# Hybrid encoder step on one core: expert rows added to the tokens on chip, instead of written to DRAM and gathered

## The chip, the core and the metric

The kernel runs on one core of a Trainium2 chip. The metric is the device time of one execution in microseconds (us). Beside it stands the span of a profiled execution, from its first to its last instruction. Engines: PE (TensorE), DVE (VectorE), ACT (ScalarE), POOL (GpSimd), SP (SyncE, which here only starts DMAs).

## What is computed

One layer for 256 prompt tokens, 64 sample tokens and 16 meta tokens of width 1024, all float32: a projection, attention and a recurrent branch, a merge, a layer norm, and then a mixture of 16 experts of which each of the 320 tokens uses two. The change lies in the experts:

```python
combine = jnp.sum(jax.nn.one_hot(e_idx, N_EXPERTS, dtype=jnp.float32) * top_w[..., None], axis=1)
y = jnp.zeros((n, D_MODEL), jnp.float32)
for e in range(N_EXPERTS):
    h = jax.nn.silu(xt @ w_gate[e]) * (xt @ w_up[e])
    y = y + combine[:, e:e + 1] * (h @ w_down[e]).astype(jnp.float32)
...
z_p = layer_norm(ALPHA * z_p + hier_moe(z_p, ...), ln2_g[l], ln2_b[l])
```

The kernel computes each expert only for the tokens that chose it: `FIRST` = 64 rows, and `REST` = 32 more where an expert has more than 64 tokens (in this input two experts do, the ones numbered 1 and 10). Overflow beyond 96 rows has code of its own that this input doesn't enter.

## The kernel before

The program is written engine by engine, with semaphores; no scheduler orders it. Up to about 333 us it computes the projections, attention, the recurrence, the first layer norm (written to `z1_dram`) and the routing: for each expert a list of token numbers, `index_i`, and for each token the two places (`place`, `slot_i`) where its expert rows will stand.

Then come 15 rounds of a pipeline, one per expert, and a last one for expert 15 (`LAST`). `SP` streams each expert's three weight matrices of 2 MB (`w_gate`, `w_up`, `w_down`) into one of three slots: the loads of gate and up of expert i wait until PE has turned the hidden rows of expert i-3, the load of down until the down products of i-3 are done. `POOL` gathers 96 token rows per expert from DRAM (`gather`), three experts ahead.

In round i PE runs, in this order (`round_of` of the tensor block): `hidden(i)` (16 gate and 16 up products, float32, 64 rows each, two at a time on two column halves of the array), `down(i-1)` (8 products 512 wide), `turn(i+1)` (8 transposes of the next expert's token rows into banks 0 and 1), `rest(i)` if the expert has more than 64 tokens, and `turn_hidden(i)`. The hidden products use three banks in turn (`HB`). ACT does the tanh of the gate and, in `rows_out`, copies the down products out of PSUM and writes them to `y_dram` ("expert_rows") with two DMAs. DVE finishes the silu, copies the transposed rows (`columns`) and the transposed hidden rows (`hidden_columns`).

`y_dram` has 96 rows per item. Rows that no token writes must be zero or at least finite, so POOL zeroes them early, at about 71 to 82 us, with 22 DMAs (lines 731 to 735), and ACT zeroes expert 15's.

At the end POOL waits until all rows are written (lines 772 to 778) and gathers, for each of three token tiles, the two expert rows of each token (line 782); DVE adds them with their weights (line 1861). Expert 15 already takes another way: DVE builds a 128x384 matrix of weights that says which row belongs to which token (line 1852), PE turns it (`turn_own`) and multiplies it with expert 15's rows (`add_last`, line 1097, float32), and DVE adds the result (line 1878). Then comes the second layer norm, whose scale and shift rows (`ln2_g`, `ln2_b`, broadcast to 128 partitions) were loaded at about 313 us.

Of the kernel before, what the change touches and what calls it, by code (L numbers as in the profile page):

```python
# [7 lines left out]
F32 = mybir.dt.float32  # L8
F32R = mybir.dt.float32r
# [6 lines left out]
P = 128  # L16
# [59 lines left out]
def const_layout():  # L76

    cols, at = {}, 0
    for name, n in (("ident", P), ("ones", P), ("eps", 1), ("before", P), ("cos", 3 * HALF), ("sin", 3 * HALF),
                    ("iota_cap", CAP), ("iota_item", NITEM), ("iota_ov", NOV), ("expert", NE),  # L80
                    ("tie", 4), ("token", 3), ("valid", 3)):
# [8 lines left out]
def constants():  # L90
# [26 lines left out]
    put("eps", EPS)  # L117
    return c
# [131 lines left out]
def build(nc, t, outs):  # L250
    (y_prompt, y_sample, meta_k, meta_v, win_k, win_v, conv_p, h_p, new_k, new_v, conv_s, h_s) = outs
    with ExitStack() as ctx:
# [11 lines left out]
        with ExitStack() as under:  # L264
# [13 lines left out]
            attn_high = lower("attn_high", 4 * NTOK)  # L278
        slots = sb("expert_slots", [P, 3 * EXP])
# [6 lines left out]
        slot_i = sb("slot_i", [P, 2, 3], I32)  # L286
# [77 lines left out]
        xg = [ea.take(D) for _ in range(3)]  # L364
        xT = [ea.take(KD, CAP) for _ in range(3)]
        yo = [ea.take(512) for _ in range(3)]
        th_a, hid_a, hT_a = ea.take(256), ea.take(256), ea.take(256)
        th_b, hid_b, hT_b, yo_b = ea.take(P), ea.take(P), ea.take(P), ea.take(256)

        own_rows = [xg[2][:, 384 * k:384 * k + 384].rearrange("p (j h c) -> p j h c", h=2, c=FIRST) for k in range(2)]
        own_T = xT[2].rearrange("p k c -> p (k c)")[:, 0:NTOK]
        own_y = yo[2]
# [6 lines left out]

        fin = Area(slots, 2 * EXP, 3 * EXP)
        yg = [[fin.take(D) for _ in range(2)] for _ in range(3)]
# [24 lines left out]
        place = sm.take(12)  # L407
        own = sm.take(2, 3)
        idle = sm.take(1)
        exi, exo = rt.take(15), rt.take(15)  # L410
        g_top, tie_top, slot_f = rt.take(3), rt.take(3), rt.take(6)
# [21 lines left out]
        TB, HB, TH, YB, BB = banks[0:2], banks[2:5], banks[5], banks[6], banks[7]  # L433

        SUM = [[banks[0], banks[1]], [banks[3], banks[4]], [banks[5], banks[7]]]

        z1_dram = nc.dram_tensor("z1_rows", [NTOK, D], F32, kind="Internal")
        y_dram = nc.dram_tensor("expert_rows", [NITEM * CAP, D], F32, kind="Internal")
# [41 lines left out]
        zeroed, zero_out = sem("zeroed"), sem("zero_out")  # L480
# [10 lines left out]
        ya_full, ya_made = sem("ya_full"), sem("ya_made")  # L491
        y_out = [sem(f"y_out{i}") for i in range(3)]
# [3 lines left out]
        yb_full, yb_made, yb_out = sem("yb_full"), sem("yb_made"), sem("yb_out")  # L496
        y_written = sem("y_written")
        la_full, la_tanh, la_half, la_made = [sem(f"last_hidden_{n}") for n in ("full", "tanh", "half", "made")]
        lt_full, lt_made, ly_full, ly_made = [sem(f"last_{n}") for n in ("turned", "turned_made", "down", "down_made")]
# [184 lines left out]
        def _(pool):  # L684
# [46 lines left out]
            for i in range(NE):  # L731
                pool.dma_start(y_dram[CAP * i + FIRST:CAP * (i + 1), :], zeros).then_inc(zero_out, 16)
# [1176 lines left out]
```

## Time and profile before

| | us |
|---|---|
| median of 3 runs | 624.0 (620.52 to 624.64) |
| profiled execution, its own time | 623.38 |
| its span | 620.3 |
| PE busy / DVE / ACT / POOL | 513.8 / 250.8 / 149.7 / 66.9 |
| mean granted TensorE clock | 0.927 |

The profiled execution has 3.1 us outside its span. Busy shares are averages over very different stages: the expert rounds run from 340 to 597 us, and the last 20 us belong to DVE.

### The profile page before, as it was taken

What the parts mean: (1) busy time and instruction counts of PE and PEld (TensorE: products, weight loads), DVE (VectorE), ACT (ScalarE), POOL (GpSimd) and SP (SyncE); (2) the same over time, 40 slices, a digit from 0 to 9 for tenths busy, and PEclk for the clock granted to TensorE, in tenths of its full rate; (3) what the DMA queues carried; (4) which work ended last, traced back from release to release, by engine and by line L of the source; (5) the groups of instructions that cost most, each with busy time, mean ns of one, the idle gap of its engine ahead of it and who ended that gap; (6) DMA issues with size and microseconds to landing.
All of it is one profiled execution on the core that took longest, in us unless ns stands there. A gap on an engine that the chain in (4) does not pass through costs nothing.

```text
span 620.3 us, 9275 instructions
## 1 busy us (share of the span) xinstructions
PE 513.8 (83%) x3600; PEld 394.0 (64%) x3601; DVE 250.8 (40%) x526; ACT 149.7 (24%) x283; POOL 66.9 (11%) x87
## 2 busy tenths in 40 slices
PE   4789978999989897999952999889997799787740
PEld 1789965988989897988652555546554455354410
DVE  2936956789464444414334111111120121111187
ACT  3435349775534422001010010000000010000010
POOL 4151730000000000000004300000000000000210
PEclk9999979999999997999955899999998899999795
DMA  8227891424257645495293299999999999999642
GB/s 227 98 73 216 230 309 42 136 70 137 69 166 279 234 166 173 155 402 215 92 412 109 96 392 365 396 408 406 393 386 403 399 403 422 409 424 423 230 106 85
DMA packets 55212, 157.47 MB, mean 254 GB/s; under 512 B 3558, under 2 KB 36034, under 8 KB 51076
## 3 DMA queue, kind: packets, MB, share of 16 engines
q1 hardware_dynamic: 46464, 135.11, 58.0%
q0 software_dynamic: 4896, 13.92, 7.7%
q10 hardware_dynamic: 3812, 7.88, 3.4%
q8 instruction: 29, 0.48, 0.3%
q14 instruction: 11, 0.09, 0.0%
HBM read 145.10 MB, written 11.78 MB: 253 GB/s over the span
## 4 chain that ended last, share of the span: by engine, by line
PE 60%; DMA 21%; DVE 7%; issue 4%; ACT 4%; SPq 2%; DVEq 1%; POOL 0%; POOLq 0%; ACTq 0%
PE bank L1043 21%; DMA expert_slots<-in_w_up 11%; PE bank L850 7%; PE bank L851 7%; PE bank L852 7%; PE bank L1004 7%; DMA expert_slots<-in_w_branch_rnn 3%; PE bank L1036 2%; SPq L606 2%; DMA expert_slots<-in_w_in 2%; DMA z_rows<-work 2%; PE bank L831 2%; PE bank L832 1%; PE bank L833 1%; DVE work L1445 1%
## 5 line engine op out<-in xcount | busy, mean ns | idle before, releaser
L1043 PE MATMUL bank<-expert_slots,work 128*64 128x256 f32 (+3 forms) x1584 | 191.9, 415 | 30.8 <-DMA expert_slots<-in_w_gate 9.4
L1043 PEld LDWEIGHTS bank<-expert_slots,work 128*64 128x64 f32 (+1 forms) x1584 | 110.8, 139 | 100.7 <-issue 46.3
L850 PE MATMUL bank<-z_high,weights_high 128*128 128x320 f32 (+1 forms) x320 | 101.6, 317 | 7.6 <-DVE weights_low L555 5.2
L852 PE MATMUL bank<-z_high,weights_low 128*128 128x320 f32 (+1 forms) x320 | 100.9, 315 | 0.0
L851 PE MATMUL bank<-z_low,weights_high 128*128 128x320 f32 (+1 forms) x256 | 79.5, 310 | 0.0
L555 DVE TENSOR_TENSOR weights_low<-expert_slots,weights_high 128x1024 fp32r<-128x1024 f32 (+1 forms) x54 | 61.1, 1157 | 38.1 <-ACT weights_high L549 37.9
L850 PEld LDWEIGHTS bank<-z_high,weights_high 128*128 128x128 f32 x320 | 61.8, 193 | 9.1 <-DVE weights_low L555 5.9
L1802 DVE SCALAR_TENSOR_TENSOR work<-work,bank 128x256 f32<-128x256 f32 (+1 forms) x18 | 7.3, 407 | 147.3 <-ACT work L1350 141.5
L549 ACT CAST weights_high<-expert_slots 128x1024 fp32r<-128x1024 f32 (+1 forms) x54 | 52.2, 987 | 48.2 <-PE bank L852 15.9
L852 PEld LDWEIGHTS bank<-z_high,weights_low 128*128 128x128 f32 x320 | 61.7, 193 | 0.0
L851 PEld LDWEIGHTS bank<-z_low,weights_high 128*128 128x128 f32 x256 | 48.0, 188 | 0.0
L1350 ACT ACTIVATE work<-bank 128x256 f32<-128x256 f32 x16 | 6.2, 384 | 170.4 <-PE bank L1043 170.4
L1004 PE MATMUL bank<-expert_slots,work 128*128 128x256 f32 (+1 forms) x192 | 41.9, 380 | 1.1 <-DVE work L1669 1.1
L752 POOL DMA_INDIRECT work<-z_rows,index_i x16 | 14.8, 923 | 235.1 <-PE bank L1036 166.4
L1004 PEld LDWEIGHTS bank<-expert_slots,work 128*128 128x128 f32 (+1 forms) x192 | 32.9, 172 | 9.8 <-DVE work L1669 1.4
L1796 DVE COPY work<-bank 128x384 f32<-128x384 f32 x32 | 16.4, 553 | 51.0 <-PE bank L1036 51.0
L1036 PEld LDWEIGHTS bank<-const,work 96*128 96x128 f32 x128 | 15.8, 207 | 16.8 <-issue 16.8
L831 PE MATMUL bank<-weights_high,z_high 128*128 128x256 f32 (+1 forms) x72 | 21.2, 295 | 3.1 <-DVE z_low L1457 1.6
L1036 PE MATMUL bank<-const,work 96*128 96x96 f32 x128 | 18.5, 290 | 5.0 <-DMA work<-z_rows,index_i 5.0
L851 PE MATMUL bank<-rnn_low,weights_high 128*128 128x320 f32 x64 | 21.6, 337 | 0.0
L832 PE MATMUL bank<-weights_low,z_high 128*128 128x256 f32 (+1 forms) x72 | 21.0, 292 | 0.0
L833 PE MATMUL bank<-weights_high,z_low 128*128 128x256 f32 (+1 forms) x72 | 20.9, 290 | 0.0
(264 smaller groups left out, 567.5 us busy)
## 6 DMA issues: line engine op xcount, KB each, us to landing
expert_slots<-in_w_gate SPq DMA_DIRECT2D x16, 2048.0 KB, 22.4
expert_slots<-in_w_up SPq DMA_DIRECT2D x16, 2048.0 KB, 28.1
expert_slots<-in_w_down SPq DMA_DIRECT2D x15, 2048.0 KB, 24.0
expert_slots<-in_w_in SPq DMA_DIRECT2D x19, 1024.0 KB, 5.3
expert_slots<-in_w_branch_rnn SPq DMA_DIRECT2D x4, 1024.0 KB, 6.4
expert_slots<-in_w_out SPq DMA_DIRECT2D x4, 1024.0 KB, 5.1
expert_rows<-work ACTq DMA_DIRECT2D x30, 128.0 KB, 8.4
expert_rows<-work POOLq DMA_DIRECT2D x6, 384.0 KB, 9.6
```

Source lines behind the costliest of these rows:

```text
L549: nc.scalar.copy(high[n % AHEAD][:, ks, :], raw[u % RING][:, ks, cols]).then_inc(high_made, 1)
L555: nc.vector.tensor_tensor(low[u % RING][:, ks, cols], raw[u % RING][:, ks, cols], high[n % AHEAD][:, ks, :], ALU.subtract)\
L831: nc.tensor.matmul(b[0:n, 0:256], zh[:, k, z], wh[:, k, :], start=(k == 0), stop=False)
L832: nc.tensor.matmul(b[0:n, 0:256], zh[:, k, z], wl[:, k, :], start=False, stop=False)
L833: mm = nc.tensor.matmul(b[0:n, 0:256], zl[k // 4][:, k % 4, z], wh[:, k, :], start=False, stop=(k == KD - 1))
L850: nc.tensor.matmul(o, wh[:, k, :], xh, start=(k == 0), stop=False)
L851: nc.tensor.matmul(o, wh[:, k, :], xl, start=False, stop=False)
L852: mm = nc.tensor.matmul(o, wl[:, k, :], xh, start=False, stop=(k == kk - 1))
L1004: mm = nc.tensor.matmul(b[0:n, 256 * q:256 * q + 256], merged[:, k, P * j:P * j + n], w[:, k, :], start=(k == 0), stop=(k == KD - 1))
L1036: mm = nc.tensor.transpose(TB[h][:, k * CAP:k * CAP + CAP], cols[:, 4 * h + k, :], ident[0:CAP, 0:CAP])
L1043: mm = nc.tensor.matmul(bank[m * j:m * j + m, cols], lhsT(k), rhs(k, j), start=(k == 0), stop=(k == kk - 1))
L1796: cp = V.tensor_copy(xT[s][:, 4 * h:4 * h + 4, :], TB[h][:, 0:4 * CAP].rearrange("p (k c) -> p k c", c=CAP))
```

## The change

Nothing of the experts' output goes to DRAM any more. After the down product of an expert (two halves of 64 rows, one for each half of the 1024 columns, in one bank), ACT rounds the bank to float32r (`y_high`) and DVE makes the rounded difference (`low_part`), so that the sum of the two parts is nearly the float32 value. For each expert POOL makes a 0/1 matrix (`own_of`) that says which of its rows belongs to which token, from two rows per token (`slot_rows`) that PE and ACT spread over the partitions once. PE multiplies the 0/1 matrix with both parts (`add_tile`: for each of three token tiles 4 float32r products 512 wide on 64 partitions, the two row halves of the array alternating), into the two banks `SUM` for all tiles. DVE multiplies by the token's weight for this expert and adds to the residual rows (`add_sum`, two instructions per tile). The sums of expert i are made in round i+2.

To free banks, the hidden products now use one bank. To free memory, two of the three buffers of gathered token rows lie where the norm rows were, so the norm rows are fetched only after expert 14, as one row each, and spread by four PE products with one partition, before `hidden(LAST)`. In a round `turn(i+1)` now stands ahead of `down(i-1)`. In `rest` the down product takes 64-row tiles 512 wide (half of its rows are zeros) and its sums are made at once, PE waiting for DVE to the end.

```diff
-            for i in range(NE):
-                pool.dma_start(y_dram[CAP * i + FIRST:CAP * (i + 1), :], zeros).then_inc(zero_out, 16)
...
+            def own_of(i, s):
+                code = cst("lane")
+                for h in range(2):
+                    nc.gpsimd.tensor_scalar(same, slot_rows[:, 0, :], -float(CAP * i), code[:, h:h + 1], ALU.add, ALU.is_equal)\
+                        .then_inc(same_made, 1)
+                    nc.gpsimd.tensor_scalar(own[s][:, h, :], slot_rows[:, 1, :], -float(CAP * i), code[:, h:h + 1], ALU.add, ALU.is_equal)\
+                        .then_inc(same_made, 1)
+                    pool.wait_ge(same_made, 4 * own_of.n + 2 * h + 2)
+                    nc.gpsimd.tensor_tensor(own[s][:, h, :], own[s][:, h, :], same, ALU.add).then_inc(own_half, 1)
+                    pool.wait_ge(own_half, 2 * own_of.n + h + 1)
+                nc.gpsimd.tensor_copy(w_own[s], w_table[:, :, i]).then_inc(own_made, 1)
...
+            for i in range(1, NE):
+                if i + 2 < NE:
+                    pool.wait_ge(xt_full, i)
+                    gather(i + 2, (i + 2) % 3)
+                if i >= 3:
+                    pool.wait_ge(sum_free, 3 * (i - 2))
+                own_of(i, i % 3)
...
+            def add_tile(into, own_s, parts, j):
+                n = min(P, own_s.shape[-1] - P * j)
+                for w in range(2):
+                    for h in range(2):
+                        half = slice(FIRST * h, FIRST * h + FIRST)
+                        mm = nc.tensor.matmul(into[h][0:n, :], own_s[half, P * j:P * j + n], parts[half, w, :], start=(w == 0), stop=(w == 1))
+            def add(i, s, j):
+                if j == 0:
+                    pe.wait_ge(low_y, i + 1)
+                    pe.wait_ge(own_made, i + 1)
+                wait_past(pe, sum_free, 3 * i + j)
+                add_tile(SUM, own_first(s), y_parts, j).then_inc(sum_full, 1)
...
-                tiles(BB, slice(0, 256), lambda k: hT_b[:, REST * k:REST * k + REST],
-                      lambda k, j: w_down[s][:, k, 256 * j:256 * j + 256], KF, REST).then_inc(yb_full, 1)
+                tiles(BB, slice(0, 512), lambda k: hT_b[:, k, :],
+                      lambda k, j: w_down[s][:, k, 512 * j:512 * j + 512], KF, FIRST).then_inc(yb_full, 1)
+                pe.wait_ge(low_yb, b + 1)
+                pe.wait_ge(own_made, i + 1)
+                wait_past(pe, sum_free, summed)
+                for j in range(3):
+                    if j == 1:
+                        pe.wait_ge(rest_sum_free, 3 * b + 1)
+                    add_tile(REST_SUM[j], own[s][:, 1, :], yr_parts, j).then_inc(rest_sum_full, 1)
+                pe.wait_ge(rest_sum_free, 3 * b + 3)
...
+            for j in range(3):
+                add(LAST - 2, (LAST - 2) % 3, j)
             down(LAST - 1, 2, NE // 3 - 1)
+            for j in range(3):
+                add(LAST - 1, (LAST - 1) % 3, j)
...
+            pe.wait_ge(norm2_in, 32)
+            for i in range(2):
+                if i:
+                    pe.wait_ge(norm2_made, 2)
+                for h in range(2):
+                    nc.tensor.matmul(TB[h][:, :], ones[0:1, :], gb[0:1, i, 512 * h:512 * h + 512], start=True, stop=True)\
+                        .then_inc(norm2_full, 1)
             hidden(LAST, 0, NE // 3, la_full)
...
-                for h in range(2):
-                    act.dma_start(dst, yo[s][FIRST * h:FIRST * h + FIRST, :]).then_inc(y_out[s], 16)
+                nc.scalar.copy(y_parts[:, 0, :], YB[:, :]).then_inc(high_y, 1)
...
+            def low_part(parts, bank, high, n, made):
+                dve.wait_ge(high, n)
+                stt(parts[:, 1, :], bank[:, :], 1.0, parts[:, 0, :], ALU.mult, ALU.subtract).then_inc(made, 1)
+            def add_sum(into, full, count, s, j, done=None):
+                n = OUT_ROWS[j]
+                dve.wait_ge(full, count)
+                for h in range(2):
+                    half = rows[0:n, j, 512 * h:512 * h + 512]
+                    inst = stt(half, into[h][0:n, :], w_own[s][0:n, j:j + 1], half, ALU.mult, ALU.add)
...
-                alone(stt(rows[0:n, j, :], yg[j][k][0:n, :], weight[k][0:n, j:j + 1], rows[0:n, j, :], ALU.mult, ALU.add))
```

PE, one round of the loop over experts (the second of its three copies). Before: hidden, down, turn, and the load of the word that says whether the expert has a rest (`rest` and turn_hidden follow).

```order
L1043 MATMUL bank<-expert_slots,work 64x256 x32
L1043 MATMUL bank<-expert_slots,work 64x512 x8
L1036 MATMUL bank<-const,work 128x96 x8
L507 ISA
L507 TENSOR_LOAD ctrl_i
```

In the changed kernel (its line 1060 is `add_tile`, 1051 `tiles`, 1044 `turn`, 1099 `turn_hidden`):

```order
L1051 MATMUL bank<-expert_slots,work 64x256 x16
L191 REGISTER_ALU
L1060 MATMUL bank<-y_parts,own_tokens 128x512 x4
L1051 MATMUL bank<-expert_slots,work 64x256 x16
L191 REGISTER_ALU
L1060 MATMUL bank<-y_parts,own_tokens 128x512 x4
L1044 MATMUL bank<-const,norm_rows 128x96 x8
L1051 MATMUL bank<-expert_slots,work 64x512 x8
L191 REGISTER_ALU
L1060 MATMUL bank<-y_parts,own_tokens 128x512 x4
```

Three groups of 4 products are new, and the 8 transposes moved ahead of the down product.

PE, the body of `rest` in the same round, before:

```order
L1043 MATMUL bank<-expert_slots,work 32x128 x64
L1107 MATMUL bank<-const,work 128x128
L1043 MATMUL bank<-expert_slots,work 32x256 x16
L1116 UNCONDITIONAL_BRANCH
L1066 MATMUL bank<-const,work 128x128 x2
```

And in the changed kernel (line 1120 is the transpose, 1131 and 1133 are waits for DVE):

```order
L1051 MATMUL bank<-expert_slots,work 32x128 x64
L1119 REGISTER_ALU
L1120 MATMUL bank<-const,work 128x128
L1051 MATMUL bank<-expert_slots,work 64x512 x8
L191 REGISTER_ALU
L1060 MATMUL bank<-y_rest_parts,own_tokens 128x512 x4
L1131 ISA
L1060 MATMUL bank<-y_rest_parts,own_tokens 128x512 x4
L1060 MATMUL bank<-y_rest_parts,own_tokens 64x512 x4
L1133 REGISTER_ALU
L1137 UNCONDITIONAL_BRANCH
L1099 MATMUL bank<-const,work 128x128 x2
```

The 16 products 256 wide became 8 of 512, and three groups of sums with waits between and behind them stand ahead of the hidden transposes.

## Rows read from the trace of the kernel before

**Rows 1.** Page, the chain that ended last, by engine.
```profile
PE 60%; DMA 21%; DVE 7%; issue 4%; ACT 4%; SPq 2%; DVEq 1%; POOL 0%; POOLq 0%; ACTq 0%
```
**Rows 2.** Stretches: busy us per engine, PEclk, DMA share, GB/s.
```profile
440.00:455.00 15.00, 14.11 (x105) 7.83 (x101) 2.29 (x5) 1.53 (x3) 0.92 (x1) 1.00 1.03 400
575.00:590.00 15.00, 10.45 (x69) 5.93 (x67) 2.62 (x10) 1.40 (x3) 4.79 (x6) 0.77 0.61 224
```
**Rows 3.** Waits 350 to 625 us: total, times, longest.
```profile
PE bank L1043 <- DMA expert_slots<-in_w_gate: 9.4, 4, 2.9
...
PE bank L1043 <- DMA expert_slots<-in_w_up: 6.1, 4, 1.7
```
**Rows 4.** Page, DMA issues: queue, count, KB each, us to landing.
```profile
expert_rows<-work ACTq DMA_DIRECT2D x30, 128.0 KB, 8.4
```
**Rows 5.** Timeline, PE at 82 us and ACT at 85 us.
```profile
82.45 1.43 PE L868 MATMUL bank<-const,expert_slots 128*128 128x128 f32 x12
...
85.32 1.04 ACT L549 CAST weights_high<-expert_slots 128x1024 fp32r<-128x1024 f32 x1 [5.86 <-DMA expert_slots<-in_w_in]
```
**Rows 6.** The w_in load (L588) issued at 75.3 us, then those issued 60.6 to 67.9.
```profile
DMA to landing us min/median/max: 10.0/10.0/10.0
...
DMA to landing us min/median/max: 5.1/5.5/5.8
```
**Rows 7.** Timeline of PE, a round: start, us, line, shape, count.
```profile
431.02 10.56 PE L1043 MATMUL bank<-expert_slots,work 128*64 128x256 f32 x80 [0.97 <-DVE work L1796]
...
443.76 10.56 PE L1043 MATMUL bank<-expert_slots,work 128*64 128x256 f32 x80 [0.89 <-DVE work L1796]
```
**Rows 8.** Timeline of PE, two products of neighbours and a 64-partition one.
```profile
119.12 0.31 PE L851 MATMUL bank<-z_low,weights_high 128*128 128x320 f32 x1
119.26 0.31 PE L852 MATMUL bank<-z_high,weights_low 128*128 128x320 f32 x1
119.50 0.49 PE L900 MATMUL bank<-expert_slots 64*128 64x128 f32 x4
```
**Rows 9.** Timeline of PE, the sums of the last expert.
```profile
597.46 2.99 PE L1097 MATMUL bank<-work 64*128 64x512 f32 x12 [0.82 <-ACT work L1412]
```
**Rows 10.** Timeline of PE, the rest of expert 1.
```profile
363.99 3.70 PE L1043 MATMUL bank<-expert_slots,work 128*32 128x128 f32 x128
...
369.54 1.93 PE L1043 MATMUL bank<-expert_slots,work 128*32 128x256 f32 x32 [0.47 <-DVE work L1816]
```
**Rows 11.** Groups by form: busy us, mean ns (DVE; ACT from 350 us; POOL).
```profile
L1878 DVE TENSOR_TENSOR work<-work,bank 128x512 f32<-128x512 f32 x4 | 2.5, 670 | 0.0
...
L1356 ACT COPY work<-bank 128x512 f32<-128x512 f32 x15 | 8.8, 586 | 49.8 <-PE bank L1043 49.8
...
L749 POOL TENSOR_SCALAR work<-work 128x1024 f32<-128x1024 f32 x2 | 5.6, 2808 | 0.0
```
**Rows 12.** Timeline of PE, rounds 4 and 5.
```profile
397.90 1.08 PE L1043 MATMUL bank<-expert_slots,work 128*64 128x256 f32 x8 [0.89 <-DVE work L1796]
...
414.02 0.86 PE L1043 MATMUL bank<-expert_slots,work 128*64 128x256 f32 x5 [0.89 <-DVE work L1796]
416.95 11.81 PE L1043 MATMUL bank<-expert_slots,work 128*64 128x256 f32 x75 [2.07 <-issue]
```
**Rows 13.** Timeline of all engines from round 14's end to the last sums.
```profile
569.06 0.39 PE L1066 MATMUL bank<-const,work 128*128 128x128 f32 x2
...
571.50 3.71 PE L1043 MATMUL bank<-expert_slots,work 128*64 128x512 f32 x16 [2.06 <-issue]
...
580.01 9.33 PE L1043 MATMUL bank<-expert_slots,work 128*64 128x256 f32 x64
...
596.73 0.59 ACT L1412 COPY work<-bank 128x512 f32<-128x512 f32 x1 [6.96 <-PE bank L1077]
...
601.01 1.29 DVE L1878 TENSOR_TENSOR work<-work,bank 128x512 f32<-128x512 f32 x2
```
**Rows 14.** Timeline of PE, one-partition products at the start.
```profile
4.67 7.19 PE L812 MATMUL bank<-norm_rows,const 1*128 1x512 f32 x8 [4.67 <-DMA const<-in_const]
```

More of the change, by code:

```diff
@@ L117, in constants @@
     put("eps", EPS)
+    lane = row % FIRST
+    put("lane", np.stack([lane, np.where(lane < REST, FIRST + lane, -1e6)], axis=1))
     return c
@@ L1123, in round_of @@
                     i = 3 * n + s
-                    hidden(i, s, n, ha_full)
+                    adds = not first or s == 2
+                    hidden(i, s, n, ha_full, (i - 2, (s + 1) % 3) if adds else None)
+                    turn(i + 1, (s + 1) % 3, n + (s + 1) // 3)
                     if not (first and s == 0):
                         down(i - 1, (s - 1) % 3, n if s else n - 1)
-                    turn(i + 1, (s + 1) % 3, n + (s + 1) // 3)
-                    maybe_rest(i, s, n)
+                    if adds:
+                        add(i - 2, (s + 1) % 3, 2)
+                    maybe_rest(i, s, n, 3 * (i - 1) if adds else 0)
                     turn_hidden(ha_made, i + 1, hta_full)
             turn(0, 0, 0)
+            pe.wait_ge(slots_made, 2)
             round_of(0, True)
@@ L1147, in _ @@
             with pe.If(has > 0):
-                rest(0, NE // 3, b + count, last=True)
+                rest(LAST, 0, NE // 3, b + count, 3 * (count + LAST), last=True)
             turn_hidden(la_made, 1, lt_full)
             down_last()
-            add_last()
+            pe.wait_ge(own_made, NE)
+            pe.wait_ge(norm2_made, 4)
+            pe.wait_ge(low_ly, 1)
+            for j in range(3):
+                add_tile(SUM_LAST[j], own[0][:, 0, :], y_parts, j).then_inc(last_sum[j], 1)
         @block.scalar
@@ new lines, in round_of @@
+                    if not (first and s == 0):
+                        low_part(y_parts, YB, high_y, i, low_y)
+                    maybe_rest(i, s)
+                    hidden_columns(i + 1)
+            round_of(0, True)
+            with dve.Fori(1, NE // 3) as n:
+                round_of(n, False)
+            for j in range(3):
+                add_first(LAST - 2, (LAST - 2) % 3, j)
+            low_part(y_parts, YB, high_y, LAST, low_y)
+            for j in range(3):
+                add_first(LAST - 1, (LAST - 1) % 3, j)
```

297 lines of the change are left out of this document (138 added, 159 removed).

## The prediction, made before the changed kernel was run

> **What bounds the kernel now.** I read the page's chain first: PE has 60% of it and DMA 21% [rows 1]. The table of stretches says where: from 350 to 575 us the DMA engines are full, at 400 GB/s in the row shown, and from 575 us on the load drops to 224 GB/s and TensorE's granted clock to 0.77 [rows 2]. The list of waits puts a number on the fight between the two: in all the expert rounds PE waited for gate and up weights 9.4 + 6.1 = 15.5 us [rows 3]. None of it lies in the rounds of [rows 7] and [rows 12]: in the first half of the rounds PE has weights in hand and sets the pace itself. So PE has about 15 us to spare in the rounds, and not more. Last I read the timeline of the tail: round 14 ends at 569.45, the last down product of the loop at 575.2, expert 15's hidden products run from 580.0 to 589.3, and DVE begins the last sums at 601.0 [rows 13]; from there it is 19.3 us to the end of the span, all DVE and the store.
>
> **Part 1, the zeroing is gone.** The load of projection weights that was issued at 75.3 us, in the midst of the 22 zeroing DMAs, took 10.0 us to land, its neighbours 5.1 to 5.8 [rows 6]. ACT waited 5.86 us for it [rows 5], and its next copy out of PSUM (86.3 us), which PE needed, could otherwise have begun at 82.6, when PE had left this product and gone on [rows 5]. From there on ACT and PE are a chain without slack. I take -3.7 us; bounds 0 and -5.9, the whole wait.
>
> **Part 2, the sums in a round.** Each round gets 12 float32r products 512 wide. Two neighbours of 320 columns start 0.14 us apart in [rows 8], and 0.146 over a longer run of such starts, so 512 columns cost 0.234. They use 64 partitions each in turns. In the sums of the last expert 12 float32 instructions of this shape (two per product, each with two passes) took 2.99 us with the drain [rows 9]; one after another they would need 12 x 0.43 = 5.1, so the halves do run side by side. One tile is then 2 x 0.234 = 0.47 us, with the seams 0.50; bounds 0.43 (at full clock) and 0.94 (no overlap at all). Three tiles: 1.5 us.
>
> A clean round now lasts 443.76 - 431.02 = 12.74 us [rows 7]. In it 0.97 us are a wait for `columns`, because the transposes come last; they now stand ahead of the down product, and I take 0.8 of it as saved. 12.74 - 0.8 + 1.5 = 13.45 us. DVE gets 6 adds and one rounding, 7 x 0.67 = 4.7 us a round, ACT nothing longer than its copy of 0.59 [rows 11]; both have room. The two banks of sums are freed between the pieces of the round, so these waits are covered.
>
> POOL's price isn't in the trace. The nearest row is 2.81 us for 1024 columns of one operation [rows 11], 0.88 us for 320. Six such and a small copy are 5.5 to 6.5 us an expert; if each had the price of two passes, 11 us. It decides only when an expert's matrix and its gather take longer than a round, about 13 us, because the matrix is started one round after the buffer is freed and is used two rounds later. I take it as hidden.
>
> **Part 3, the rest of an expert.** Before, from 364.0 to 371.5, 7.4 us [rows 10]. After: 3.7 for gate and up, 1.8 for silu and the transpose (369.5 - 367.7, as before), 3.45 for 8 down products 512 wide instead of 1.9, then a chain that nothing covers: ACT 0.6, DVE 0.7, a tile 0.75 with start and drain, DVE 1.35 for its two adds, a second tile 0.75, the third beside it, DVE 2 x 1.35. That is 16.0 us, +8.6. There are two. The first, in round 1, also holds back the loads of gate and up 4, which wait for that round's end: the queue runs dry some 8 us longer than now. This costs the stream what the expert rows gave back: 30 DMAs of 128 KB [rows 4] are 3.9 MB, 9.8 us at 400 GB/s. So the stream of weights ends about where it does now, and the question is only whether PE keeps up.
>
> **Part 4, the rounds together.** From the start of the rest of expert 1 at 364.0: 16.0 + 0.4 for turn_hidden gives 380.4; 13 rounds of 13.45 are 174.9; the second rest 16.0. Rounds 4 and 5 took 16.1 and 17.0 us before (starts 397.90, 414.02, 431.02), 7.7 us over the clean round, with PE stopped for 2.07 us in the first products of one of them though the profile shows nothing that it waits for [rows 12, 7]. It is the first time that PE goes through this part of its program while the DMA engines are full; as nothing in the change takes that away I keep 7.7 (bounds 0 and 15). Sum: 579.0 at round 14's end, against 569.45: **+9.6**. PE hardly waits for weights in this sum: the 15.5 us of slack are used up by 2 x 8.6 + 12 x 0.7.
>
> **Part 5, the tail.** Before, 31.6 us from round 14's end to the last sums [rows 13]. After, from 579.0: the sums of expert 13 can only start when its rounded parts are there (2.0), then tile, add, tile, add, tile, 0.5 to 0.75 and 1.35 in turn: 6.6 until PE is free. Down 14: 3.45. ACT 0.6, DVE 0.7, and tile, add, tile, add, tile again: 5.8. That is 594.9. The branch past the overflow code 1.3 (PE started 1.3 us after its release there before). The norm rows, fetched when ACT has copied down 14, have landed by then; four products of one partition in two pairs, the second pair after ACT's copies. 8 instructions took 7.19 us at 1.2 GHz at the start of the kernel [rows 14]; in two pairs at full clock 3.5 and the copies 0.6: 4.1, bounds 3.5 and 8. So 600.3. Hidden 15: 9.3 before, after an idle stretch at a low clock [rows 13, 2]; 7.1 clean; I take 8.4. From its end to the end of the last down product 7.3 as before (589.3 to 596.7): 616.0. Rounding on ACT and DVE and the first tile 2.1: 618.1. Before, 601.0. What is removed here, six gathers and six adds of DVE, lay beside expert 15's products and gave 4 us at most. Tail: 39.1 against 31.6, **+7.5**.
>
> **Sum.** 620.3 - 3.7 + 9.6 + 7.5 = 633.7 us of span, 636.8 with the 3.1 outside, 13.4 above the profiled execution's 623.4. The median of the runs is 0.6 above that execution, so I forecast 637.
>
> **A rule of the skill.** Product 852 starts at 119.26 and the next one, on 64 partitions, at 119.50, where neighbours of one shape are 0.14 apart: a change of shape costs 0.1 us there [rows 8]. The Trainium skill, "TensorEngine Tiling (Array Packing)", section Tiling Modes, says that a change of tiling mode (not just of the tile) drains the engine. By that rule each of the three groups in a round would pay a drain going in and one coming out; the trace agrees in sign, for one kind of change.
>
> **Rivals.**
> A, the stream stays the bound, and the kernel isn't slower. If a round takes 13.1 us, if the 7.7 us of rounds 4 and 5 go because the DMA engines are less full, and the rest overlaps to 12 us, PE reaches round 14 ahead of its weights, at about 566 instead of 579; in the tail the norm products and the clean clock save 4 more. 637 less 13 less 4 less 3 for smaller bounds of the tiles: 617. For it: 3.9 MB fewer, and PE had 15.5 us of waits. Against: the first rest starves the queue early. It decides where PE's rounds, rests included, take less than the 15.7 us that 6.3 MB per expert need at 400 GB/s [rows 2].
> B, the array drains at each change between 64-column and 64-partition products. A product's record is 0.31 us long and the next starts 0.14 later [rows 8], so a drain is up to 0.17 us; 6 per round and as many again in the rests and the tail's groups are 1.0 us a round: about 90 changes, 12 to 14 us. 650.
> C, GpSimd is the bound: at 16 us an expert the rounds take that long, 2.5 more for 10 of them. For it: the price is from one row only. Against: that row would have to be off by 2.5. 655.
>
> **Chances.** Forecast 0.62 (630 to 645), A 0.17, B 0.13, C 0.08. The range: low end, all small bounds together (-7.7 of part 4, -3 in tiles, -2 in the tail) and half of A, 623; high end B, 650. A change of 1% is about what a measurement of this kernel can tell from none. Faster by over 1% (under 617.8): 0.09; within 1%: 0.17, the slower half of A and the low edge of the forecast; slower: 0.74.
>
> **What would show it.** In the trace after: ACT's wait at 80 us gone and all stages 3.7 us earlier; rounds of 13.45 us, three groups of 0.5; rests of 16 us with DVE and PE in turns; PE's waits for weights in the last rounds near zero while the DMA share falls below 1; round 14's end near 575 (579 less 3.7), the last sums 39 us later. Wrong if PE still waits for gate weights in rounds 12 to 14 (A), if a group takes over 0.7 us (B), or if PE waits for `own_made` (C).

## The result, and the profile after

The changed kernel takes 766.6 us (median of 4 runs, 761.0 to 771.8) beside 624.3 for the kernel before on the same chip (4 runs): ratio 1.225, with a 95% interval from 1.220 to 1.230. It is 142 us slower; I had forecast 13 and a range that ended at 650. The sign was right, for a reason that was not the large one.

First the page of the changed kernel: the DMA queue that brings instructions, and the chain that ended last by engine.

```profile
q8 instruction: 58, 0.95, 0.5%
...
PE 69%; issue 15%; DVE 7%; DMA 5%; ACT 3%; DVEq 0%; SPq 0%; POOLq 0%; ACTq 0%
```

The same line of the queues on the page of the kernel before:

```profile
q8 instruction: 29, 0.48, 0.3%
```

Read the chain against [rows 1]: DMA fell from 21% to 5%, so the stream of weights no longer bounds anything, and "issue", time in which the engine waits for nothing that the profile shows, rose from 4 to 15%. 15% of 770 us are some 115. The queue line names a suspect: twice as many packets of instructions, though by the two pages PE ran only 5% more products (3781 records against 3600).

Waits of PE from 340 us on, changed kernel (total us, times, longest):

```profile
PE bank L1099 <- issue: 50.1, 11, 5.7
PE bank L1051 <- issue: 39.3, 4, 13.5
PE bank L1060 <- DVE work L1859: 9.0, 6, 1.5
```

89 us of PE's idle time end with no releaser, and the waits for weights of [rows 3] are gone from the list. The timeline of PE shows one round of the loop, which answers to [rows 7] (start, us, line, shape, count, and in brackets the idle time ahead of it with what ended it):

```profile
443.24 6.46 PE L1051 MATMUL bank<-expert_slots,work 128*64 128x256 f32 x32
449.63 0.73 PE L1060 MATMUL bank<-y_parts,own_tokens 64*128 64x512 f32 x4
450.30 3.67 PE L1051 MATMUL bank<-expert_slots,work 128*64 128x256 f32 x32
453.90 0.73 PE L1060 MATMUL bank<-y_parts,own_tokens 64*128 64x512 f32 x4
454.57 1.13 PE L1044 MATMUL bank<-const,norm_rows 96*128 96x96 f32 x8
455.63 3.65 PE L1051 MATMUL bank<-expert_slots,work 128*64 128x512 f32 x16
459.21 0.73 PE L1060 MATMUL bank<-y_parts,own_tokens 64*128 64x512 f32 x4
464.83 0.69 PE L1099 MATMUL bank<-const,work 128*128 128x128 f32 x2 [4.89 <-issue]
476.93 4.99 PE L1051 MATMUL bank<-expert_slots,work 128*64 128x256 f32 x32 [11.42 <-issue]
```

The reader is to see two things. A tile of sums, L1060, takes 0.66 to 0.67 us from its start to the next product's (449.63 to 450.30; the 0.73 of its record has the modelled end in it). And PE stands still where it jumps over the code of `rest` to the hidden transposes (L1099): in eleven of the loop's twelve rounds, for 4.8 to 5.7 us in nine of them and 1.0 and 3.1 in the other two (in the twelfth the rest is run). Where the loop over three rounds begins again it stands still for 11.4 us. The clock pays too: the first 32 records after a stall took 6.46 us here, at a granted clock of 0.55, the next 32 took 3.67 at 1.00. The stretch of the long stall:

```profile
465.40:476.90 11.50, 0.12 (x1) 0.18 (x1) 0.42 (x1) 0.00 (x0) 4.57 (x5) 0.50 1.00 362
```

PE busy 0.12 us, the granted clock at 0.50 (1.2 GHz), the DMA engines full with weights that PE is not using yet.

### The profile page after: what moved, and what is told of

It reads as the page before. It is cut to its first block, busy times and chain, and to the rows that moved or that the text cites. A ratio compares the mean times of both kernels' runs of the same rounds, so it can differ in the third digit from the quotient of the medians.

```text
span 769.9 us, 9811 instructions
## 1 busy us (share of the span) xinstructions
PE 586.0 (76%) x3781; PEld 418.5 (54%) x3782; DVE 323.4 (42%) x636; ACT 152.8 (20%) x287; POOL 168.1 (22%) x169
## 4 chain that ended last, share of the span: by engine, by line
PE 69%; issue 15%; DVE 7%; DMA 5%; ACT 3%; DVEq 0%; SPq 0%; POOLq 0%; ACTq 0%
PE bank L1051 28%; PE bank L854 6%; PE bank L855 6%; PE bank L856 6%; PE bank L1008 5%; PE bank L1060 5%; DMA expert_slots<-in_w_branch_rnn 3%; PE bank L1044 2%; DVE work L1859 2%; DMA z_rows<-work 1%; PE bank L835 1%; PE bank L836 1%; PE bank L837 1%; PE bank L1099 1%; DVE work L1478 1%
## 5 line engine op out<-in xcount | busy, mean ns | idle before, releaser
L1051 PE MATMUL bank<-expert_slots,work 128*64 128x256 f32 (+2 forms) x1552 | 217.6, 450 | 41.9 <-issue 40.4
L1051 PEld LDWEIGHTS bank<-expert_slots,work 128*64 128x64 f32 (+1 forms) x1552 | 115.6, 151 | 129.8 <-issue 103.0
L1859 DVE SCALAR_TENSOR_TENSOR work<-bank,work 128x512 f32<-128x512 f32 (+1 forms) x108 | 75.6, 742 | 147.7 <-PE bank L1060 147.7
L756 POOL TENSOR_SCALAR work<-work,const 128x320 f32<-128x320 f32 x32 | 43.5, 1361 | 224.9 <-DVE work L1859 223.1
L1099 PE MATMUL bank<-const,work 128*128 128x128 f32 x32 | 10.0, 410 | 57.2 <-issue 50.1
L758 POOL TENSOR_SCALAR own_tokens<-work,const 128x320 fp32r<-128x320 f32 x32 | 43.3, 1352 | 0.9
L1060 PE MATMUL bank<-y_parts,own_tokens 64*128 64x512 f32 (+1 forms) x192 | 36.6, 464 | 9.0 <-DVE work L1859 6.0
L1099 PEld LDWEIGHTS bank<-const,work 128*128 128x128 f32 x32 | 4.2, 185 | 63.9 <-issue 61.4
L1060 PEld LDWEIGHTS bank<-y_parts,own_tokens 64*128 64x128 f32 (+1 forms) x192 | 15.3, 194 | 34.0 <-issue 23.2
```

Source lines behind the costliest of these rows:

```text
L756: nc.gpsimd.tensor_scalar(same, slot_rows[:, 0, :], -float(CAP * i), code[:, h:h + 1], ALU.add, ALU.is_equal)\
L758: nc.gpsimd.tensor_scalar(own[s][:, h, :], slot_rows[:, 1, :], -float(CAP * i), code[:, h:h + 1], ALU.add, ALU.is_equal)\
L1051: mm = nc.tensor.matmul(bank[m * j:m * j + m, cols], lhsT(k), rhs(k, j), start=(k == 0), stop=(k == kk - 1))
L1060: mm = nc.tensor.matmul(into[h][0:n, :], own_s[half, P * j:P * j + n], parts[half, w, :], start=(w == 0), stop=(w == 1))
L1099: mm = nc.tensor.transpose(TH[:, P * h:P * h + P], hid_a[:, P * h:P * h + P], ident)
L1859: inst = stt(half, into[h][0:n, :], w_own[s][0:n, j:j + 1], half, ALU.mult, ALU.add)
```

## The experiments

(That count is too high, by 50 to 60 in every kernel: I had taken the float32 transposes for four instructions too, while the trace has one record of a transpose where it has two of a product. With two instructions each, the bodies are 1559 and 1631. The lengths below and in the expectations are by the first count; their order and the 32, 48 and 96 that are added are right.) Rival G: the branch over `rest` itself is dear, because it now follows other waits. Rival C: GpSimd.

**e1_trim.** Both rests of this input lie in the second of the three copies of the round, or ahead of the loop; so the rest code can be left out of the other two copies and the work done stays the same.

```diff
-                    maybe_rest(i, s, n, 3 * (i - 1) if adds else 0)
+                    if first or s == 1:
+                        maybe_rest(i, s, n, 3 * (i - 1) if adds else 0)
```

> The changed kernel, with PE's code for the rest of an expert left out of the first and third of the three copies in the loop over experts (no expert that these copies serve has a rest in this input, so that code never ran; the other engines are unchanged). PE's loop gets some 660 of 1681 instructions shorter. Theory F (PE's loop no longer stays in its instruction store, so its code is fetched again in every iteration, and PE stands still with nothing to wait for): the idle stretches with no releaser (5 us ahead of the hidden transposes, 11 to 13 us at one round in three) go in all three copies, instruction DMA packets fall from 58 to about 30, and the time is 630 to 645 us. Rival G (the branch past the rest now stands behind a wait for DVE, so that the load of the two control words and the branch lie open, 5 us a round): the stretch goes in the two copies that have no branch any more and stays at 5 us in the second copy; the 11 to 13 us stretches stay; about 725 us. Rival C (GpSimd's matrices set the pace): no change, 766 us.

Measured: 671.6 us (667.3 to 672.8), ratio to before 1.073 (1.065 to 1.080). 95 us are gone, with nothing removed but code that was never run. PE's waits from 340 us on, and the queue:

```profile
PE bank L1051 <- issue: 9.8, 2, 5.3
PE bank L1060 <- DVE work L1860: 9.0, 6, 1.5
...
q8 instruction: 29, 0.48, 0.3%
```

The packets are back at 29. The second copy still has its branch, and PE stands still at it in no pass, which speaks against G. But 671.6 is not my 637; what is left is taken up below.

**e2_pad96, e3_pad32, e4_shift96.** The other way round: products that are never run are put into the kernel before, behind the branch of `rest`. e2 puts 12 (48 instructions) into each of two copies of the loop body (body 1711), e3 4 into each (1647), e4 24 into expert 0's rest ahead of the loop (body 1615, shifted by 96).

```diff
-            def rest(s, n, b, last=False):
+            def rest(s, n, b, last=False, pads=0):
...
+                for _ in range(pads):
+                    nc.tensor.matmul(BB[0:REST, 0:P], xT[s][:, 0, FIRST:CAP], w_gate[s][:, 0, 0:P], start=True, stop=True)
```

> The kernel before, with 24 float32 products (96 instructions) more in PE's loop body, inside the branch for the rest of the first and third copy, so that they never run in this input. Theory F: the body grows from 1615 to 1711 instructions, more than the changed kernel's 1681; the loop is fetched anew in each iteration and the time rises by 30 to 140 us over 624, instruction packets rise from 29 to 50 or more. Rivals G and C: no change, 624 us.

> The kernel before, with 8 float32 products (32 instructions) more in the same places, never run: a body of 1647 instructions, which by my count still ends before the 16 KB block that the changed kernel's body reaches into. Theory F in the form that whole blocks count: no change, 624 us, 29 or 30 instruction packets. If F holds with a limit on the plain length below 1647: slower as in the kernel with 96 more. Rivals G and C: no change.

> The kernel before, with 24 float32 products (96 instructions) more ahead of the loop, in the branch for the rest of expert 0 (never run in this input): the body keeps its 1615 instructions but lies 96 later, so that by my count it ends in the block that the changed kernel's body also reaches into. Theory F with whole blocks that count: slower, like the kernel with 96 more in the body. F with the plain length of the body that counts: no change, 624 us. Rivals G and C: no change.

Measured: e2 671.1 us, ratio 1.078 (1.069 to 1.087); e3 669.9 (one run); e4 624.2 (one run). The queue of instructions and PE's largest waits without a releaser, first e3, then e4:

```profile
q8 instruction: 58, 0.95, 0.6%
...
PE bank L1043 <- issue: 35.4, 8, 7.8
PE bank L1066 <- issue: 28.6, 8, 4.4
```

```profile
q8 instruction: 31, 0.51, 0.3%
...
PE bank L1066 <- issue: 16.8, 5, 4.1
```

32 instructions that PE never executes cost the kernel before 45 us (e3 is one run; the four of e2 say the same). The packets come where the theory has them: in e3 nine from 447 to 508 us and nine from 508 to 570, each about a pass of the loop, and in the kernel before none from 470 to 575. Between e3 and e2 there is no difference: it is a step, not a slope. e4 has stalls too, the 16.8 us above, but all five lie between 350 and 439 us, ahead of the loop and in its first pass; later passes have none, and the time is that of the kernel before. So the length of the loop's body counts, and the kernel before stood at the edge, by at most 32 instructions: the limit lies between 1615 and 1647 by my first count, 1559 and 1591 by the corrected one.

I first read e4 as saying that the place of the body doesn't count. It doesn't show that. In the first pass of the kernel before, PE breaks off without a releaser in the hidden products of three rounds in a row, after 11, 8 and 5 records. [rows 12] has the last two; this is the first:

```profile
384.59 1.50 PE L1043 MATMUL bank<-expert_slots,work 128*64 128x256 f32 x11 [0.98 <-DVE work L1796]
386.30 9.42 PE L1043 MATMUL bank<-expert_slots,work 128*64 128x256 f32 x69 [0.21 <-issue]
```

A record of a product stands for two instructions, the weight load and the product, so from copy to copy the break comes 6 instructions earlier. Suppose that the breaks are the ends of packets of 256 instructions. Then a copy is 2 x 256 + 6 = 518 long and three are 1554, which agrees with the corrected count. As the first break comes some 25 instructions into the loop, the body begins about 230 into a packet and ends within some ten instructions of the end of its seventh. 32 more reach into an eighth, and so do the bodies of e2 and of the changed kernel; the body of e4, moved by 96, begins about 70 into a packet and needs seven again. "No more than seven packets stay" fits every run here as well as a limit on the plain length does. A shift of about 16 would tell the two apart; none was run.

The Trainium skill, "Runtime: NRT & Kernel Launch", section "Instruction fetch mechanics", gives PE a store of 2048 instructions that is refilled in blocks of 256, and says that a branch out of the present window forces a fetch. The trace agrees on the blocks (0.95 MB in 58 packets are 16 KB each) and on the stall. On the size the runs show only that a body of 1647 (1591 by the corrected count) no longer stays, though it is well short of 2048. Seven packets that stay, and room for one that is being fetched, would make eight, which is 2048; that reading isn't tested.

**e10_trim_one.** The rest code out of the first copy alone (body 1351).

```diff
-                    maybe_rest(i, s, n, 3 * (i - 1) if adds else 0)
+                    if first or s != 0:
+                        maybe_rest(i, s, n, 3 * (i - 1) if adds else 0)
```

> The changed kernel with the rest code left out of the first copy of the round alone: PE's loop body 1351 instructions (1681 in the changed kernel, 1021 with both copies out, 1615 in the kernel before). Theory F as a limit between 1615 and 1647: the loop stays in the store, about 30 instruction packets instead of 58, and the time is that of both copies out, 671 to 675. Rival (each instruction of the body costs something in every pass): half the way, 719.

Measured: 683.2 us (two runs), 30 packets. A step again, not half the way; but 12 us above e1, where I had allowed 4. PE's waits without a releaser, from 340 us on (timeline):

```profile
398.80 5.90 PE L1051 MATMUL bank<-expert_slots,work 128*64 128x256 f32 x32 [3.99 <-issue]
...
435.95 5.61 PE L1051 MATMUL bank<-expert_slots,work 128*64 128x256 f32 x26 [5.24 <-issue]
...
457.42 0.69 PE L1099 MATMUL bank<-const,work 128*128 128x128 f32 x2 [5.63 <-issue]
```

The third row is new against e1: the third copy's jump in the first pass, over code that has not been brought yet. With the slow products behind it (5.20 us for 3.67), this makes 7 to 8 us of the 12.

**e5_before_trim.** The same trimming of both copies in the kernel before.

> The kernel before, with the rest code left out of the first and the third copy of the round in PE's loop (both rests of this input lie in the second copy or ahead of the loop, so the work done is the same; the loop body shrinks from 1615 to about 1021 PE instructions). The theory of the instruction store (F): the loop of before already fits, so only the first pass through it gets shorter: 3 of its stalls instead of 5, 4 to 8 us less, 616 to 620 us. If the length of a body that fits cost nothing even in the first pass: 624, no change. If before paid anything per pass for its length: under 605.

(By a later count the body is 945 instructions.) Measured: 623.2 us, ratio 0.9998 (0.996 to 1.004): nothing, and F had said 4 to 8 less. The stalls of the first pass did go, but for one of 0.5 us; this is PE's timeline where [rows 12] had them, and 15 us behind it:

```profile
398.39 10.56 PE L1043 MATMUL bank<-expert_slots,work 128*64 128x256 f32 x80 [0.89 <-DVE work L1797]
411.13 10.56 PE L1043 MATMUL bank<-expert_slots,work 128*64 128x256 f32 x80 [0.89 <-DVE work L1797]
...
442.42 8.79 PE L1043 MATMUL bank<-expert_slots,work 128*64 128x256 f32 x48 [2.06 <-DMA expert_slots<-in_w_up]
```

PE arrives earlier and waits for weights instead (17.8 us of such waits for 15.5, and the products behind them run slower, 8.79 us for 48 records that take 7.11 at best): the kernel before is bound by its stream in these rounds. So the 7.7 us that I kept for rounds 4 and 5 are indeed a first fetch of code, but in the kernel before they were free.

**e7_one_part.** From here the base is e1_trim, 671.6 us. One of the two rounded parts is left out of each sum (the output lacks the low parts).

```diff
-                for w in range(2):
+                for w in range(1):
```

> The changed kernel with the shortened loop (671.6 us), leaving out the products with the rounded-off low parts: a tile of sums is 2 products instead of 4 (it leaves out that part of the output's precision; ACT and DVE still make both parts). If a tile costs its columns (my 0.234 us per pair), the spacing of 0.66 us falls to 0.43 and the whole by 50 tiles x 0.23 = 11 us: 660. If a change between the forms of the array costs it (rival B: two changes a tile), 0.66 falls by less than 0.1: 667 or more.

Measured: 652.4 us (two runs), 19 us less. A tile's spacing is now 0.435 us:

```profile
448.00 3.67 PE L1051 MATMUL bank<-expert_slots,work 128*64 128x256 f32 x32
451.60 0.51 PE L1060 MATMUL bank<-y_parts,own_tokens 64*128 64x512 f32 x2
452.04 3.67 PE L1051 MATMUL bank<-expert_slots,work 128*64 128x256 f32 x32
```

A tile fell by 0.66 - 0.435 = 0.225 us, my 0.234 for a pair within 4%. So two pairs are 0.45 of the 0.66, and 0.21 us do not depend on the number of products. I put them down to the change of form going in and coming out, about 0.1 each, as in [rows 8]; that fits, but no run takes the changes away. Then both theories had a part, and the columns twice that of the drain. Between the two profiled executions lie 22.4 us. The 54 tiles explain 12 of them. The two stalls of the first pass, 9.8 us in e1, are here 0.9 and 1.3, and the down product of the tail took 4.84 us for 6.08 and the last one 3.65 for 5.35. 2.0 us were there ahead of the router, where nothing differs, and 3.3 us of waits for up weights have come back. Why a body of 973 instructions has a mild first pass and one of 1021 a dear one I haven't settled.

**e6_norm_dma and e11_tail_order.** The tail. e6 brings the second norm's rows to all partitions by two DMAs, in place of four PE products and four copies; e11 adds to it another order after the loop.

```diff
-                act.dma_start(gb[0:1, i, :], t[name]).then_inc(norm2_in, 16)
+                act.dma_start(gb[:, i, :], t[name].to_broadcast([P, D])).then_inc(norm2_in, 16)
```

```diff
-            for j in range(3):
-                add(LAST - 2, (LAST - 2) % 3, j)
+            add(LAST - 2, (LAST - 2) % 3, 0)
             down(LAST - 1, 2, NE // 3 - 1)
+            for j in range(1, 3):
+                add(LAST - 2, (LAST - 2) % 3, j)
```

> The changed kernel with the shortened loop (671.6 us), and the second norm's scale and shift rows brought to all 128 partitions by two DMAs of 512 KB instead of by two one-row DMAs, four PE products and four ACT copies. Theory N (the tail's excess over my 39 us sits in what PE does and waits for between the last sums and expert 15): PE goes from 618.8 to the hidden products of expert 15 with 1 to 4 us of branch in place of 11.8 us, and the DMAs land beside them: 660 to 664. Rival (the wait of 3.65 us ahead of the norm products is a fetch of PE's code and stays, and the array is cold after it): 667. If the DMAs land later than PE is through with expert 15: 671 or more.

> The changed kernel with the shortened loop and the norm rows by DMA (667.2 us), and after the loop the down product of expert 14 put between the first and the second tile of expert 13's sums. PE then does not stand still twice for 1.5 us while DVE adds. By the waits alone: 3.0 us less, 664. If the clock, which stood at 0.62 in this down product, also rises because PE is idle for less: 5 us less, 662. If ACT's rounding of expert 14 now waits for expert 13's sums to be read (it needs the buffer of parts), 1.5 of it come back: 665.5.

Measured: e6 667.2 us (663.2 to 668.4), ratio 1.066; e11 661.5 (659.2 to 662.6), ratio 1.059. In e6, PE from the last sums to expert 15 and on:

```profile
619.98 1.22 PE L1060 MATMUL bank<-y_parts,own_tokens 64*128 64x512 f32 x4 [1.51 <-DVE work L1847]
624.83 9.65 PE L1051 MATMUL bank<-expert_slots,work 128*64 128x256 f32 x64 [3.63 <-issue]
636.85 0.69 PE L1099 MATMUL bank<-const,work 128*128 128x128 f32 x2 [2.36 <-issue]
638.05 6.41 PE L1110 MATMUL bank<-expert_slots,work 128*64 128x512 f32 x16 [0.52 <-DVE work L1917]
```

8 us of PE time went and only 4.4 came off. The wait of 3.6 us without a releaser stayed (the jump over the overflow code), and the work behind it grew, 9.65 us for 9.00 and 6.41 for 5.35: so far the rival was right. But from round 14's end to the last sums e6 is 6.8 us shorter than e1; the other 2.4 were lost ahead of that, 2.0 of them ahead of the router, where the kernels are the same. That its 667 came out is partly luck. e11 matched the value with the clock by its number alone. Of the two waits of 1.5 us that were to go, only one did (five waits for the adds for six), another grew from 1.42 to 2.09, and the first down product fell from 6.07 to 5.34: together PE comes to expert 15 1.5 us sooner. The other 3.7 are expert 15's own products, 8.71 us for 9.65 and 3.65 for 6.41. The three kernels ran on three chips and the intervals of neighbours overlap (e1 1.065 to 1.080, e6 1.059 to 1.073, e11 1.053 to 1.065), so both steps rest on the timelines more than on the times.

**e8_zero_back and e9_late_zero.** The zeroing. e8 puts the 22 DMAs and ACT's wait back into e1_trim; e9 lets the kernel before start them later.

```diff
-            pool.wait_ge(conv_made, 2)
+            pool.wait_ge(conv_made, KD)
```

> The changed kernel with the shortened loop (671.6 us), and the 22 zeroing DMAs, the memset ahead of them and ACT's wait for them put back where they stood in the kernel before (nothing reads what they write). My part 1: the w_in load at 75 us takes 10 us again, ACT waits 5.9 us for it, all stages come 3.7 us later (router products at 304.4 instead of 300.7): 675.3. Rival: the load is late for another reason and nothing moves: 671.6. If the 4.6 us by which the router products came earlier than in before all come from it: 676.2.

> The kernel before, with the 22 zeroing DMAs started when all eight blocks of the convolution are made (about 90 us) instead of two of them (71 us); from 95 to 115 us the DMA engines were idle in the kernel before. Theory (part 1: the zeroing delays one load by 4 to 5 us, and PE and ACT are a chain from there): the w_in load lands in 5 to 6 us, ACT's wait at 80 us falls from 5.9 to about 1, everything comes 3.7 to 4.6 us earlier, and the stream of weights, which bounds the experts, starts as much earlier: 620. Rival: the stream does not start earlier or the zeroing only hits another load: 624.

Measured: e8 675.7 us (672.8 to 678.0), 4.1 above e1; e9 619.4 us (12 runs), ratio to before 0.992 (0.988 to 0.996), some 5 us less. ACT's rounding that waited for the w_in load, in e8 and in e9; [rows 5] has it for the kernel before:

```profile
85.26 1.04 ACT L556 CAST weights_high<-expert_slots 128x1024 fp32r<-128x1024 f32 x1 [6.33 <-DMA expert_slots<-in_w_in]
```

```profile
79.34 1.05 ACT L549 CAST weights_high<-expert_slots 128x1024 fp32r<-128x1024 f32 x1 [0.95 <-DMA expert_slots<-in_w_in]
```

Each of the two steps alone is small (the intervals of e8 and e1 overlap, and e9 is less than 1% below the kernel before), but all the traces agree. The transposes ahead of the router start at 304.1 to 308.8 us in the six kernels with the zeroing early, and at 297.7 to 302.9 in the eight with it late or gone: 6.1 us apart in the mean. So the direction of part 1 is right and the 3.7 too small. The zeroing needs no removal: started some 15 us later, beside DMA engines that were 10% busy from 94 to 115 us in the kernel before, it costs nothing that these times show.

**e12_late_zero_trim.** e9 with the rest code out of the first and the third copy as well.

> The kernel before with late zeroing and with the rest code out of the first and third copy of the loop (body 945 PE instructions). As the shortened loop alone gave nothing in the kernel before (623.2 against 624.0; PE then waited for weights instead), the stream bounds it: the same as late zeroing alone, 620. If with the earlier start PE and not the stream bounds the rounds, the shorter first pass is worth up to 4 us more: 616.

Measured: 618.3 us (6 runs, 615.6 to 619.8), ratio 0.988 (0.984 to 0.993). By the medians 1 us below e9, and the intervals overlap; both beat the kernel before by about 1%, and the changed one by far. PE's waits for weights, 10.6 and 12.9 us, show that the stream is still the bound:

```profile
PE bank L1043 <- DMA expert_slots<-in_w_gate: 12.9, 6, 3.1
...
PE bank L1043 <- DMA expert_slots<-in_w_up: 10.6, 5, 3.0
```

## Why the prediction was wrong, point by point

**The step that failed is in part 4**, "the rounds together": I added 13 rounds of one length and kept 7.7 us for a part of the program that PE goes through "for the first time". I had read the stall rightly as code being reached for the first time, and never asked whether it would stay the first time only. The question had rows to be asked from: 4 idle stretches without a releaser, and 29 packets of instructions, of which the loop needed none from 470 to 575 us. With the body beyond the limit, each of the four passes fetches its code again (nine packets from 476.9 to 550.9 us in the changed kernel, a whole pass), and 766.6 - 671.6 = 95 us of the 142 come from that alone (e1). About 80 of them are PE's waits without a releaser (89.4 against 9.8); the rest fits the slow products behind each stall, which I did not try apart. My bounds for the term were 0 and 15, and no rival had it.

**Part 1** had the mechanism right and the size a little low: -3.7 predicted (bound -5.9), +4.1 when put back (e8), about -5 when only moved in the kernel before (e9), and 6.1 us at the router in the mean of the traces.

**Part 2.** The product's price was right (0.234 against 0.225 per pair), the seams were mis-sized: a tile takes 0.66 us, not 0.50. By my reading of e7 this is rival B's drain, at 0.1 us where B had 0.17. A clean round, read from e1:

```profile
451.25 3.67 PE L1051 MATMUL bank<-expert_slots,work 128*64 128x256 f32 x32
...
465.47 0.87 PE L1051 MATMUL bank<-expert_slots,work 128*64 128x256 f32 x6
```

14.22 us, not 13.45. Three tiles cost 3 x 0.16 more than I had them, and the pieces of the hidden and down products, started anew after each tile, are what I take the rest for. Over 13 rounds it is 10 us. GpSimd was mis-sized without harm: 1.36 us for two operations on 320 columns, against 0.88 for one; with the copy 7.4 us an expert, hidden in a round of 14. PE never waited for its matrix, so rival C fell:

```profile
L756 POOL TENSOR_SCALAR work<-work,const 128x320 f32<-128x320 f32 x31 | 42.2, 1361 | 224.8 <-DVE work L1859 223.1
L758 POOL TENSOR_SCALAR own_tokens<-work,const 128x320 fp32r<-128x320 f32 x31 | 41.9, 1352 | 0.8
L761 POOL TENSOR_TENSOR own_tokens<-own_tokens,work 128x320 fp32r<-128x320 f32 x30 | 25.8, 859 | 2.5
```

**Part 3** was right: the second rest costs 538.75 - 507.80 - 14.21 = 16.7 us in e1, against 16.0, and PE and DVE take turns as described. I left out that the granted clock is lower behind these turns (0.61 and 0.71 in the first 32 records): the round behind each rest is 2.5 and 1.7 us longer.

**Part 4, the remainder in e1.** From expert 1's hidden transposes to those of expert 14: 597.35 - 376.70 = 220.7 us, against my 198.6. The rounds give 10 of the difference, the first pass through the loop 14.9 instead of 7.7, the clock behind the rests 4.2, the rest 0.7: 22.1 with rounding.

**Part 5, the tail**, from round 14's end to the last sums: 53 us in e1, against 39.1. This timeline of e1 answers to [rows 13]:

```profile
605.64 6.08 PE L1051 MATMUL bank<-expert_slots,work 128*64 128x512 f32 x16
...
622.49 3.75 PE L1185 MATMUL bank<-norm_rows,const 1*128 1x512 f32 x4 [3.65 <-issue]
626.91 3.78 PE L1185 MATMUL bank<-norm_rows,const 1*128 1x512 f32 x4 [0.68 <-ACT norm_rows L1438]
630.61 9.00 PE L1051 MATMUL bank<-expert_slots,work 128*64 128x256 f32 x64
642.57 0.44 PE L1099 MATMUL bank<-const,work 128*128 128x128 f32 x2 [2.95 <-issue]
643.53 5.35 PE L1110 MATMUL bank<-expert_slots,work 128*64 128x512 f32 x16 [0.52 <-DVE work L1930]
```

Down 14 took 6.08 us for my 3.45, the branch 3.65 for 1.3, the norm rows 8.1 for 4.1 (the upper bound), the two groups of sums 2.5 more together, expert 15 and what follows 2.7 more. But for the branch and the waits for DVE, which I had at 1.35 us and which took 1.5, it is one omission: I priced the tail at full clock. The stretches say what was granted, for down 14 and for the first pair of norm products:

```profile
606.00:612.00 6.00, 5.71 (x16) 0.62 0.01 1
...
622.40:626.30 3.90, 3.75 (x4) 0.50 0.02 4
```

In the kernel before the clock stood at 0.77 in this stage [rows 2], with less waiting ahead of it than I was adding. That row should have priced the added work at 0.5 to 0.8. One reading was loose as well: I called the products of [rows 14] products at 1.2 GHz, and the granted clock reads 1.00 in that stretch. That they ran at half speed is seen only at 28 us, where products of one shape go from 0.215 to 0.115 us apart. The 0.94 us a record in the tail, at 0.50, bears it out.

Of the 47 us between e1 and the kernel before, then, the rest of expert 1 is 9, the rounds with the rest of expert 10 are 23, the tail is 22, and 4 come back from part 1: 50, beside 50.6 between the spans. Even without the code fetch the changed kernel is 35 us above my forecast, and the 15 us of slack in the stream was used up by the rounds.

**Rival A** fell because PE, even in e1, sets the pace of all its rounds: from 340 us on it waits for no weights, in the changed kernel or in e1. The reason that I gave against A, a queue starved by the first rest, would have shown as such a wait, and there is none.

## What to carry to other kernels

Count the instructions of an engine's loop body, never-taken branches included, before and after a change, and look at the packets of the instruction queue in the profile. In a kernel with a tuned loop, a few lines more can turn a fetch that happened once into one in every pass, and a wait without a releaser right behind a jump is the sign of it. A stall that is seen in the kernel before should be explained before it is carried into a sum, since what causes it decides how often it comes. And work added where an engine waits in turns with another is to be priced at the clock granted there, not at full clock.

## What was not expected of the hardware

- PE's loop of 1615 instructions was brought once (29 packets in the whole execution), and one of 1647 in every pass (58 packets), for 45 us in four passes. By the corrected count these are 1559 and 1591. Whether the limit is a length or seven whole packets is open.
- A fetch behind a jump cost 3.65 us with the DMA engines idle, in e1, and 4.8 to 5.7 in nine jumps of the changed kernel, beside the stream of weights (the engines 0.70 to 0.91 busy). The stretch of the idle case, in e1:

```profile
618.80:622.40 3.60, 0.03 (x2) 0.00 (x0) 1.40 (x2) 0.00 (x0) 0.00 (x0) 0.50 0.03 7
```

- So most of the stall is there without any load. That the load makes the rest is not shown: in e3 six jumps cost 3.7 to 4.4 us with the DMA engines at 0.95 and more, as much as the idle one. Where the loop begins again three packets come close together, and PE stood still for 10.7 to 13.5 us.
- Still open: why the first pass is dear in e1 and e10 and cheap in e7 and e5; and some 4 of the 12 us between e10 and e1.
